# The last down projection with tokens as rows, and h turned inside the up stage

## The reference

```python
def rmsnorm(x, g):
    y = xf * lax.rsqrt(jnp.mean(xf * xf, axis=-1, keepdims=True) + RMS_EPS)
    return (y * g.astype(jnp.float32)).astype(x.dtype)

def swiglu(x, w_gu, w_down):
    gate, up = jnp.split(x @ w_gu, 2, axis=-1)
    return (jax.nn.silu(gate) * up) @ w_down
...
        f = swiglu(rmsnorm(h, ffn2_g_pre[l]), ffn2_w_gu[l], ffn2_w_down[l])
        h = h + MACARON_W * rmsnorm(f, ffn2_g_post[l])
    return h
```

## Time and profile before

| | |
|---|---|
| median of 3 runs | 1247.38 us (1246.58 to 1247.57) |
| the profiled execution | 1244.26 us, its span 1242.5 us |
| TensorE busy | 1195.2 us, 96% of the span |
| ScalarE, VectorE, GpSimd busy | 445.7, 406.9, 480.2 us |
| last up group, about | 1080 to 1102 us |
| last down projection | 1102 to 1222 us |
| the tail | 1222 us to the end |

### The profile page before, as it was taken

The page is one execution under the profiler, slowest core; times in us unless marked ns, Lnnn a source line. Parts: engine busy times, 40 slices in busy tenths (PEclk is TensorE's granted clock), DMA queues, the critical chain, the costliest instruction groups (busy, mean ns, idle before and its releaser), DMA issues. The chain is left out here.

```text
span 1242.5 us, 15268 instructions
## 1 busy us (share of the span) xinstructions
PE 1195.2 (96%) x5639; PEld 984.3 (79%) x5639; DVE 406.9 (33%) x720; ACT 445.7 (36%) x675; POOL 480.2 (39%) x219
## 2 busy tenths in 40 slices
PE   8999999999998999999998988798999999999997
PEld 5888888888887688787787877687888888888886
DVE  6431312210008565655525424506422121310004
ACT  4332322331125474455343434424423232321123
POOL 2444353544445332113043733132435344354431
PEclk9999999999998999999998999898999999999999
DMA  5233233322222221112033431022233233222221
GB/s 174 85 102 101 86 100 101 94 92 101 101 86 67 68 89 64 51 52 85 20 100 104 137 116 51 17 85 68 85 102 94 92 101 101 89 97 102 93 76 68
DMA packets 83318, 108.75 MB, mean 88 GB/s; under 512 B 8686, under 2 KB 53836, under 8 KB 83276
## 3 DMA queue, kind: packets, MB, share of 16 engines
q1 hardware_dynamic: 83120, 108.14, 27.1%
q10 hardware_dynamic: 156, 0.04, 0.0%
HBM read 106.06 MB, written 2.10 MB: 87 GB/s over the span
## 5 line engine op out<-in xcount | busy, mean ns | idle before, releaser
L569 POOL TENSOR_TENSOR w_lo<-raw,w_hi 128x1024 fp32r<-128x1024 f32 x193 | 464.9, 2419 | 729.1 <-ACT w_hi L631 729.0
L1440 PE MATMUL bank<-xh,w_hi 128*128 128x512 f32 x984 | 388.1, 394 | 9.7 <-ACT xh L644 4.7
L1444 PE MATMUL bank<-xl,w_hi 128*128 128x512 f32 x984 | 385.8, 392 | 0.0
L1441 PE MATMUL bank<-xh,w_lo 128*128 128x512 f32 x984 | 385.8, 392 | 0.0
L631 ACT ACTIVATE w_hi<-raw 128x1024 fp32r<-128x1024 f32 x196 | 204.2, 1054 | 371.8 <-DMA raw<-in_ffn_w_down 167.6
L1440 PEld LDWEIGHTS bank<-xh,w_hi 128*128 128x128 f32 x984 | 186.5, 189 | 49.8 <-issue 10.3
L1444 PEld LDWEIGHTS bank<-xl,w_hi 128*128 128x128 f32 x984 | 186.1, 189 | 39.8 <-DVE xl L988 0.5
L1441 PEld LDWEIGHTS bank<-xh,w_lo 128*128 128x128 f32 x984 | 186.5, 190 | 37.6
L1440 PE MATMUL bank<-mid_hi,w_hi 128*128 (+1 forms) x352 | 137.2, 390 | 0.0
L1444 PE MATMUL bank<-mid_lo,w_hi 128*128 (+1 forms) x352 | 137.0, 389 | 0.0
L1441 PE MATMUL bank<-mid_hi,w_lo 128*128 (+1 forms) x352 | 136.9, 389 | 0.0
(11 more groups left out here) (246 smaller groups left out, 1244.1 us busy)
## 6 DMA issues: line engine op xcount, KB each, us to landing
raw<-in_ffn_w_gu SPq DMA_DIRECT2D x176, 256.0 KB, 2.9
raw<-in_ffn_w_down SPq DMA_DIRECT2D x88, 256.0 KB, 2.8
raw<-in_mix_w_in SPq DMA_DIRECT2D x48, 256.0 KB, 2.8
raw<-in_mem_w_kv SPq DMA_DIRECT2D x32, 256.0 KB, 3.2
raw<-in_mix_w_out SPq DMA_DIRECT2D x16, 256.0 KB, 2.9
raw<-in_mem_w_q SPq DMA_DIRECT2D x16, 256.0 KB, 3.1
raw<-in_mem_w_o SPq DMA_DIRECT2D x16, 256.0 KB, 2.8
x_tok<-in_x SPq DMA_DIRECT2D x4, 512.0 KB, 5.5
```

The source lines that it names most:

```text
L569: gp.tensor_tensor(w_lo[:, n % SLOTS, :], raw[:, n % SLOTS, :], w_hi[:, n % SLOTS, :].bitcast(F32), ALU.subtract).then_inc(lo_ready, 1)
L1440: pe.matmul(dst, w[0], x[0], start=start, stop=False, skip_group_check=loose)
L1441: pe.matmul(dst, w[1], x[0], start=False, stop=False, skip_group_check=loose)
L1444: return pe.matmul(dst, w[0], x[1], start=False, stop=stop, skip_group_check=loose)
```

## The change

Only the last sub-layer changes, and what its tail needs.

- **Down.** For each block, the 128 tokens of a chunk of `mid` stand still, and 512 columns of `w_down` move (`token_out`, `down_block`). Tile (t, half) is 128 tokens by 512 output features, in bank `tok_bank(t, half)`. The 22 blocks are written out in place of the loop. The last two are taken together (`down_last`): each tile is finished with both before the next one is touched, and counts up `tile_done`.
- **h.** It is turned to token rows, by 32 transposes into banks 4 to 7, inside the last up group: 16 behind its second block and 16 behind its third (`turn_h`). VectorE copies the banks to `h_tok`. For this the loops over the up groups have one turn less in this sub-layer, and the last two groups stand behind them, written out.
- **Tail.** For each tile ScalarE squares the bank and sums along the row in the same instruction (`accum_out`); VectorE multiplies the bank by 0.5 and the gain, which lies along the row. For each row of two tiles VectorE adds the two sums, ScalarE takes the root, VectorE the reciprocal, and VectorE computes (product x reciprocal) + `h_tok` for both tiles (`last_norm`). SyncE stores each tile. GpSimd has nothing in the tail, and neither has TensorE.
- **Gain.** `ffn2_g_post` no longer comes with the other gains at the start. SyncE loads it to all 128 partitions (`g_tok`, 512 KB in SBUF) behind the last weight block, when the up blocks are used up.
- `g_tok` lies where `xh` was, `out_tok` where `xl` was.

```diff
--- before.py
+++ after.py
+        def tok_bank(t, half):
+            return bank[(2 * t + half + 4) % 8]
...
-            copied = [(ocopied_a, t + 1) for t in range(TC)]
-            copied += [((ocopied_a, ocopied_v)[t % 2], (TC, 0)[t % 2] + t // 2 + 1) for t in range(TC)]
-            for n, (semaphore, count) in enumerate(copied):
-                half, t = n // TC, n % TC
-                sp.wait_ge(semaphore, count)
-                cols = slice(half * HW, (half + 1) * HW)
-                sp.dma_start(out[0, t * P:(t + 1) * P, cols], out_tok[:, t, cols]).then_inc(stored, 16)
+            sp.wait_ge(w_used, B_DOWN2)
+            sp.dma_start(g_tok[:, :], a["ffn2_g_post"][0].partition_broadcast(P)).then_inc(g_landed, 16)
+            for t in range(TC):
+                for half in range(2):
+                    sp.wait_ge(finished, 2 * t + half + 1)
+                    cols = slice(half * HW, (half + 1) * HW)
+                    sp.dma_start(out[0, t * P:(t + 1) * P, cols], out_tok[:, t, cols]).then_inc(stored, 16)
...
-            gp.wait_ge(frinv, SUBLAYERS)
-            for c in (2, 3):
-                gp.wait_ge(saved_a, c - 1)
-                gp.tensor_tensor(f_fin[:, c, :], f_saved[:, c - 1, :], rinv[:, :], ALU.mult).then_inc(normed_p, 1)
-            gp.wait_ge(normed_v, 3)
-            gp.tensor_tensor(h[:, 7, :], h[:, 7, :], f_fin[:, 7, :], ALU.add).then_inc(summed_p, 1)
...
-                    if s == SUBLAYERS - 1 and m in (2, 3):
-                        act.activation(f_saved[:, m - 1, :], out_bank(s, m)[:, :], ACT.Copy,
-                                       scale=post[:, s, m:m + 1]).then_inc(saved_a, 1)
...
+            def last_norm():
+
+                act.preload_act_table(ACT.Sqrt)
+                for t in range(TC):
+                    for half in range(2):
+                        n = 2 * t + half
+                        act.wait_ge(tile_done, n + 1)
+                        act.activation(sq[:, half, :], tok_bank(t, half)[:, :], ACT.Square,
+                                       accum_out=f_sq[:, n:n + 1]).then_inc(tile_sq, 1)
+                    act.wait_ge(tile_sum, t + 1)
+                    rms_root(root_tok[:, t:t + 1], f_ms[:, t:t + 1], D).then_inc(tile_root, 1)
...
-            post_norm(3)
-            for t in range(TC):
-                act.wait_ge(oturned, t + 1)
-                act.activation(out_tok[:, t, 0:HW], bank[4 + t][:, :], ACT.Copy).then_inc(ocopied_a, 1)
-            for t in range(0, TC, 2):
-                act.wait_ge(oturned, TC + t + 1)
-                act.activation(out_tok[:, t, HW:D], bank[t][:, :], ACT.Copy).then_inc(ocopied_a, 1)
+            last_norm()
...
+            def last_norm():
+
+                dve.wait_ge(g_landed, 16)
+                for t in range(TC):
+                    r = slice(t, t + 1)
+                    for half in range(2):
+                        n, cols = 2 * t + half, slice(half * HW, (half + 1) * HW)
+                        dve.wait_ge(tile_sq, n + 1)
+                        if half:
+                            dve.tensor_tensor(f_ms[:, r], f_sq[:, n - 1:n], f_sq[:, n:n + 1],
+                                              ALU.add).then_inc(tile_sum, 1)
+                        dve.scalar_tensor_tensor(out=out_tok[:, t, cols], in0=tok_bank(t, half)[:, :],
+                                                 scalar=LAST_SCALE, in1=g_tok[:, cols], op0=ALU.mult,
+                                                 op1=ALU.mult).then_inc(weighted, 1)
+                    dve.wait_ge(tile_root, t + 1)
+                    dve.reciprocal(rinv_tok[:, r], root_tok[:, r]).then_inc(tile_inv, 1)
+                    dve.wait_ge(tile_inv, t + 1)
+                    for half in range(2):
+                        cols = slice(half * HW, (half + 1) * HW)
+                        dve.wait_ge(weighted, 2 * t + half + 1)
+                        dve.scalar_tensor_tensor(out=out_tok[:, t, cols], in0=out_tok[:, t, cols],
+                                                 scalar=rinv_tok[:, r], in1=h_tok[:, t, cols], op0=ALU.mult,
+                                                 op1=ALU.add).then_inc(finished, 1)
...
-                with dve.Fori(0, FG // 2) as i:
+                with dve.Fori(0, FG // 2 - s // 3) as i:
                     for g in range(2):
                         group(1 + g, i)
+                if s:
+                    group(FG - 2)
+                    for n in range(2 * TC):
+                        t, half = n % TC, n // TC
+                        dve.wait_ge(h_turned, n + 1)
+                        dve.tensor_copy(h_tok[:, t, half * HW:(half + 1) * HW], bank[4 + t][:, :]).then_inc(h_saved, 1)
+                    group(FG - 1)
...
-            post_norm(3)
-            for c in (0, 1, 7, 4, 5, 6):
-                if c == 1:
-                    dve.wait_ge(saved_v, 1)
-                    dve.tensor_tensor(f_fin[:, c, :], f_saved[:, 0, :], rinv[:, :], ALU.mult).then_inc(normed_v, 1)
-                else:
-                    src = f0 if c == 0 else out_bank(3, c)[:, :]
-                    dve.scalar_tensor_tensor(out=f_fin[:, c, :], in0=src, scalar=post[:, 3, c:c + 1],
-                                             in1=rinv[:, :], op0=ALU.mult, op1=ALU.mult).then_inc(normed_v, 1)
-
-            for c in (4, 5, 6):
-                dve.wait_ge(normed_v, c)
-                dve.tensor_tensor(h[:, c, :], h[:, c, :], f_fin[:, c, :], ALU.add).then_inc(summed_v, 1)
-            for t in range(1, TC, 2):
-                dve.wait_ge(oturned, TC + t + 1)
-                dve.tensor_copy(out_tok[:, t, HW:D], bank[t][:, :]).then_inc(ocopied_v, 1)
+            last_norm()
...
-            def turn_h(t):
-
-
-                for j in range(4):
-                    pe.matmul(bank[4 + t][:, j * P:(j + 1) * P], h[:, j, t * P:(t + 1) * P], ident[:, :],
-                              start=j == 0, stop=False, skip_group_check=True)
-
-            def turn_f(c):
-
+            def turn_h(half):
+
+                if half:
+                    pe.wait_ge(h_saved, TC)
                 for t in range(TC):
-                    last = pe.matmul(bank[4 + t][:, c * P:(c + 1) * P], f_fin[:, c, t * P:(t + 1) * P],
-                                     ident[:, :], start=False, stop=c == 3, skip_group_check=True)
-                    if c == 3:
-                        last.then_inc(oturned, 1)
+                    for j in range(4):
+                        last = pe.transpose(bank[4 + t][:, j * P:(j + 1) * P],
+                                            h[:, 4 * half + j, t * P:(t + 1) * P], ident[:, :])
+                    last.then_inc(h_turned, 1)
+
+            def token_out(n, x, t, half, w, start, end):
+
+                tok, cols = slice(t * P, (t + 1) * P), slice(half * HW, (half + 1) * HW)
+                return three(tok_bank(t, half)[:, :], (x[0][:, tok], x[1][:, tok]), (w[0][:, cols], w[1][:, cols]),
+                             start, end, True)
+
+            def down_block(n, x, first, free={}):
+
+                w = weights(n)
+                for t in range(TC):
+                    if t in free:
+                        pe.wait_ge(*free[t])
+                    for half in range(2):
+                        last = token_out(n, x, t, half, w, first, False)
+                last.then_inc(w_used, 1)
+
+            def down_last(n, xs):
+
+                ws = [weights(n), weights(n + 1)]
+                for t in range(TC):
+                    for half in range(2):
+                        for k in range(2):
+                            last = token_out(n + k, xs[k], t, half, ws[k], False, k == 1)
+                        last.then_inc(tile_done, 1)
...
-                if s == SUBLAYERS - 1:
-                    pe.wait_ge(saved_v, 1)
-                    turn_h(1)
-                    pe.wait_ge(saved_a, 1)
-                    turn_h(2)
...
-                if s == SUBLAYERS - 1:
-                    pe.wait_ge(saved_a, 2)
-                    turn_h(3)
...
-                with pe.Fori(0, FG // 2) as i:
+                def up_pair(pair, i=None):
+
                     for g in range(2):
-
+                        g += 2 * pair
...
+                            if g == FG - 2 and k == 1:
+                                pe.wait_ge(up_scaled, first + 2 * FG - 1)
+                                turn_h(0)
+                            if g == FG - 2 and k == 2:
+                                turn_h(1)
+
+                with pe.Fori(0, FG // 2 - s // 3) as i:
+                    up_pair(0, i)
+                if s:
+                    up_pair(FG // 2 - 1)
+
+                def fixed(c):
+                    return mid_hi[:, c, :], mid_lo[:, c, :]
...
-            pe.wait_ge(frinv, SUBLAYERS)
-            turn_h(0)
-            for c, ready in enumerate(((normed_v, 1), (normed_v, 2), (normed_p, 1), (normed_p, 2))):
-                pe.wait_ge(*ready)
-                turn_f(c)
-
```

(6 more changed lines are left out.)

66 lines of the change are left out of this document (38 added, 28 removed).

## The result

The changed kernel takes 1235.67 us, the median of 4 runs (1233.09 to 1236.66), against 1247.47 for the kernel before beside it (4 runs, 1246.58 to 1247.60). The ratio is 0.9902, with a 95% interval from 0.9884 to 0.9920. The forecast was 1237.8. The sign came out as said, and the gain is larger: 11.8 us by the medians (12.2 by the ratio) where 9.55 was worked out. The profiled execution took 1235.89 us, its span is 1234.2.

A forecast was written before the change was run, and what follows sets the result against it. Bound: TensorE's full-clock matmul stream, then a 20.7 us tail chain. New end 1221.81 + 3.5 + 4.1 + 3.54 = 1232.95 against 1242.5, 9.55 less: median 1237.8 us, range 1235.5 to 1243.5.

The forecast's parts named there:

- its own sign: Prediction wrong unless the last down product ends about 3.5 us later and the piece behind is about 7.6, not 20.7.
- the last store: End of the span: the last store leaves as before, 3.54 us after the last compute.
- The down stream: Last down projection: 528 matmuls before and after, 0.227 us a step in token form; term 0.
- Rival (d): Down projection: token form slower, 0.083 us more for each of 176 products, 14.6 us, time 1252.4; chance 0.04.
- h turned: Last up stage: 32 transposes in the matmul stream at 0.109 us each cost 3.5 us.
- rival (a): Up stage: the clock falls at both turns of h, 5.5 us more, 1243.3; chance 0.09.
- rival (b): Up stage: transposes take two passes, 7.1 us instead of 3.5, time 1241.4; chance 0.05.
- The copies and the last two blocks: VectorE's eight copies of turned h, and down weights needed one block earlier with 3.6 us of slack: both 0.
- The new tail: Behind the last product: VectorE, 3.0 us a row against TensorE's 2.72, sets the end at E + 4.1.
- E: The end of the last product of the down projection, from which the tail's times are counted.
- low end: Forecast's favourable end: turns 3.2 and tail 3.5, given as 10.7 us less, 1236.7; the range began at 1235.5.
- rival (c): Tail: VectorE's products are held beside busy GpSimd, 5.4 us a row, end E + 13.7, time 1247.4; chance 0.03.

The follow-up runs named there:

- the second series: The changed kernel once more, no edit, beside runs of the kernel before: 1236.19 us (6 runs), ratio 0.9910.

## Where the prediction was right, and where it was off

By its own sign the prediction is wrong in one part: the piece behind the last product was to be about 7.6 us and is 5.72. The path was right, and two terms of that piece were too large, VectorE's row and the last store. The other terms came out.

**The down stream: 0, right.** 119.99 us after, 120.01 before. By the page of the kernel after, a matmul of the token form with the same operands turned about is no longer than one of the old form (group, count | busy us, mean ns | idle before):

```profile
L1456 PE MATMUL bank<-mid_hi,w_hi 128*128 (+1 forms) x176 | 68.6, 390 | 0.0
L1456 PE MATMUL bank<-w_hi,mid_hi 128*128 128x512 f32 x176 | 68.6, 390 | 0.0
```

Rival (d), 0.083 us for each product, would have been 14.6 us; there is nothing of it. The 0.31 of the earlier trace rows belongs to the start of a run behind a pause or behind small products, where it is seen here too, and not to a change of operands.

**h turned: 3.5, measured 3.57.** The nearest rows, eight transposes between products, carried over to sixteen and to 48 without a change in price. Rival (a) (the clock) and rival (b) (two passes) are each answered by a run, and each is wrong about this kernel.

**The copies and the last two blocks: 0, right.** Without the copies and turns the stream is back at its old time to 0.01 us. With them TensorE is busy for all 12.00 us around both turns, and the turns' own steps are 3.48 of the 3.57, so no wait for the copies is to be seen. The down stream lost nothing to weights that have to be there one block earlier.

**The new tail is the step that failed, in its size.** The forecast had E + 4.1 for VectorE's last result; it is E + 3.25. That VectorE and not TensorE sets this was right: two experiments moved TensorE's rows and VectorE's rows apart, and the end followed VectorE. The row was mis-sized. I put four products at 0.66 and two small operations at 0.155, with a few hundredths for waits, at 3.0. Measured from start to start on the timeline are 0.60 for the first product with the gain (1223.28 to 1223.88), 0.07 for the add of the two sums, 0.60 for the second product, 0.19 for the reciprocal and 1.33 for the last two products (1224.74 to 1226.07, where the next row starts): 2.79. The 0.66 was read from a product that reads a bank, as the two with the gain do, but whose scalar is a column in SBUF (`post`). The last two products have such a column (`rinv_tok`) and do take 0.66; the two with the gain have a constant in its place and take 0.60. That the scalar makes this difference is the reading that fits all these rows; no run varied it alone. The 0.155 is a whole duration where only the step to the next start counts, because the next operation does not need the sum. Three rows of 0.21 are 0.63. The first row ends at 1221.95 + 1.42 = 1223.37, E - 5.11, where the forecast had E - 4.85. Together 0.89, on a forecast that was E + 4.15 before it was rounded to E + 4.1.

**The last store was a term of that tail too, and it was carried over.** "The last leaves as now, 3.54 after the last compute" took the 3.54 for the price of a store. It contains 1.03 us in which SyncE was still issuing the stores of results that had become ready together. After, results come one tile at a time, the issue of the last store ends 0.36 behind the last compute, and the term is 2.47. The experiment with the turning alone has the same 0.37 with results that come one by one, in the old form of the tail. The 0.40 that is left of the difference, behind the last issue, stays open. My range gave this term no width at all, and that is most of why its low end lay too high; VectorE's last result, 3.25 where the low end had 3.5, is the rest (the turns, 3.57 where it had 3.2, work the other way). The low end holds a slip too: 3.2 + 3.5 is 10.45 less, 1236.9, and not 10.7 and 1236.7.

The sum of the differences: 0.85 + 1.07 - 0.07 for the turns = 1.85, and 9.55 + 1.85 = 11.40, against a measured 11.41. What is beyond that, in 11.8 by the medians or 10.9 in the second series, lies ahead of the changed stage, where the same kernel differs by several microseconds from run to run. These runs don't tell whether the change itself has a part in it. The markers of the other eight profiles lie between 883.08 and 888.76, on both sides of the 886.4 that the kernel before would have at its median (883.27 + 3.1, an estimate), which gives no sign of such a part but doesn't rule it out.

**The other zeros.** The load of the gain row took 4.6 us to land and was there; rival (c) did not happen, and GpSimd has no tensor work left in the tail, which was its condition. In the old tail, where GpSimd works beside them, the experiment with the turning alone has the long products again (1.85 and 1.75). No run put GpSimd's work beside the new tail.

## What to carry to other kernels

Where a normalisation follows a matrix product, choose the orientation in which the sum of the norm runs along the row, and give the last blocks tile by tile: the norm then goes under the products, and the orientation itself was free here. Size such a tail by the engine with the longest period for a row, here 2.79 us of VectorE against 2.72 of TensorE, and by the distance from one start to the next of the same instruction form, not by durations. And take the time behind the last compute apart, into the queue of issues and what stands behind the last issue, before carrying it over to a kernel that finishes its results one by one.

## What the runs showed of the hardware that I had not expected

- A long row of transposes did not lower the clock: 48 of them, 5.40 us, between products, with a granted clock of 1.00 during and behind them.
- A fp32 transpose of 128x128 costs 0.109 us in a stream, the same block as a plain fp32 product against the identity 0.224 (7.18 / 32), and the trace has two instructions for it.
- The length of the stretch at the lower clock behind a piece of small work is not fixed: behind the same norm it was 3.9, 5.3 and 6.1 us in three profiles, while the changed stage, with a granted clock of 1.00 from the marker to the last product, took 347.82 and 347.83 us.
- From one start to the next, VectorE took 0.60 us for the scalar-tensor products whose scalar is a constant, and 0.66 for those where it is a column. Where the tensors lie doesn't seem to matter for it: with the column the pair takes 1.41 to 1.42 whether h comes from SBUF or, with the last row turned late, from PSUM. No run varied the scalar alone.
- Stores that become ready together wait for SyncE, which took 0.45 us for an issue in such a queue and 0.33 for the last one when it came alone.
